# The opening of a two-layer encoder kernel: two more low halves written by DMA, two first scaled tiles on ScalarE, narrow column products among wide ones, and one column sum moved

## What is computed

```python
shift, scale, gate = split(silu(c) @ w_mod[i] + b_mod[i], 3)
h = rmsnorm(x, norm_g[i]) * (1.0 + scale) + shift
# layer 0: z, bg, cg, xh = split(h @ w_in, 4); y = depthwise width-3 conv of cg * xh
#          y = (bg * y * silu(z)) @ w_out
# layer 1: z from h @ w_in, u and v = gelu(rest); v = layernorm(v), mixed over
#          128-position chunks per head; y = (u * sv * silu(z)) @ w_out
x = x + gate * y
```

## Time and profile before

| | |
|---|---|
| median of three runs | 814.75 us |
| profiled execution, its span | 812.9 us |
| TensorE busy | 803.3 us, 99% |
| VectorE busy | 649.2 us, 80% |
| ScalarE busy | 442.6 us, 54% |
| granted TensorE clock | 1.00 until after the last product |
| DMA, first three of 40 slices (61 us) | busy share 0.9 or more |

### The profile page before, as it was taken

One profiled execution on the slowest core, in us unless ns is written; L12 is line 12 of the kernel. 1 busy time (PEld: TensorE's weight loads), 2 busy tenths in 40 slices (PEclk: granted clock), 3 DMA queues, 4 the chain that ended last, 5 costly groups with the idle time before them and its releaser, 6 DMA issues.

```text
span 812.9 us, 15224 instructions
## 1 busy us (share of the span) xinstructions
PE 803.3 (99%) x5614; PEld 752.5 (93%) x5614; DVE 649.2 (80%) x950; ACT 442.6 (54%) x624; POOL 50.9 (6%) x68
## 2 busy tenths in 40 slices
PE   9999999999999999999999999999999999999997
PEld 8779999999999999988889888899999999988896
DVE  5989999999999999898653787567888888897534
ACT  4575656565656666562332844446667677762220
POOL 1010000000000000000000000010000000000000
PEclk9999999999999999999999999999999999999999
DMA  9994566666565656587422162414555445487103
GB/s 350 366 245 131 153 185 179 184 177 190 171 196 166 202 164 198 171 315 288 160 79 79 61 250 98 134 21 143 148 155 148 125 140 148 136 303 265 52 1 104
DMA packets 39566, 137.85 MB, mean 170 GB/s; under 512 B 4336, under 2 KB 6512, under 8 KB 39536
## 3 DMA queue, kind: packets, MB, share of 16 engines
q1 hardware_dynamic: 31616, 110.64, 37.0%
q0 software_dynamic: 6912, 25.17, 16.4%
q10 hardware_dynamic: 1008, 1.66, 0.6%
HBM read 108.09 MB, written 4.19 MB: 138 GB/s over the span
## 4 chain that ended last, share of the span: by engine, by line
PE 94%; DVE 3%; issue 2%; ACT 0%; POOL 0%; POOLq 0%; DVEq 0%; ACTq 0%
PE pp L1190 11%; PE pp L1191 11%; PE pp L1192 11%; PE pp L1046 8%; PE pp L1048 7%; PE pp L1047 7%; PE p_aux L1190 7%; PE p_aux L1192 7%; PE p_aux L1191 7%; PE pp L1328 4%; PE pp L1326 4%; PE pp L1327 4%; PE p_aux L1400 2%; PE pp L1145 1%; PE pp L1062 1%
## 5 line engine op out<-in xcount | busy, mean ns | idle before, releaser
L1190 PE MATMUL pp<-h_hi,wh 128*128 128x256 f32 x280 | 79.3, 283 | 0.0
L1192 PE MATMUL pp<-h_hi,wl 128*128 128x256 f32 x280 | 79.2, 283 | 0.0
L1191 PE MATMUL pp<-h_lo,wh 128*128 128x256 f32 x280 | 79.2, 283 | 0.0
L1701 DVE TENSOR_TENSOR wl<-wt,wh 128x1024 fp32r<-128x1024 f32 x56 | 66.5, 1219 | 0.2 <-ACT wh L698 0.2
L698 ACT ACTIVATE wh<-wt 128x1024 fp32r<-128x1024 f32 x56 | 58.9, 1054 | 13.7 <-DVE wt L1682 7.6
L1190 PE MATMUL pp<-s_hi,wh 128*128 128x256 f32 x224 | 63.4, 283 | 0.0
L1191 PE MATMUL pp<-s_lo,wh 128*128 128x256 f32 x224 | 63.4, 283 | 0.0
L1192 PE MATMUL pp<-s_hi,wl 128*128 128x256 f32 x224 | 63.4, 283 | 0.0
L1192 PE MATMUL p_aux<-s_hi,wl 128*128 128x256 f32 x224 | 63.4, 283 | 0.0
L1191 PE MATMUL p_aux<-s_lo,wh 128*128 128x256 f32 x224 | 63.4, 283 | 0.0
L1190 PE MATMUL p_aux<-s_hi,wh 128*128 128x256 f32 x224 | 63.4, 283 | 0.0
(11 more groups left out here) (237 smaller groups left out, 2598.1 us busy)
## 6 DMA issues: line engine op xcount, KB each, us to landing
raw<-in_stream SPq DMA_DIRECT2D x144, 512.0 KB, 4.0
wl<-raw POOLq DMA_DIRECT2D x28, 512.0 KB, 4.5
raw_l<-in_stream SPq DMA_DIRECT2D x18, 512.0 KB, 4.6
raw_s<-in_stream SPq DMA_DIRECT2D x16, 512.0 KB, 13.6
wl_b<-raw POOLq DMA_DIRECT2D x16, 512.0 KB, 4.5
raw_m<-in_stream SPq DMA_DIRECT2D x14, 512.0 KB, 3.2
x_s<-in_xt SPq DMA_DIRECT2D x4, 512.0 KB, 6.0
w_lo_s<-raw POOLq DMA_DIRECT2D x4, 512.0 KB, 5.4
```

The source lines that it names most:

```text
L1190: pe.matmul(out, hi, hi_of(k), start=fresh and k == 0, stop=False, skip_group_check=not fresh)
L1191: pe.matmul(out, hi, lo_of(k), start=False, stop=False, skip_group_check=not fresh)
L1192: mm = pe.matmul(out, lo, hi_of(k), start=False, stop=k == 3, skip_group_check=not fresh)
L1701: dve.tensor_tensor(wl[par][:, part], wt[par][:, part], f32(wh[par][:, part]), ALU.subtract).then_inc(t_cut, 1)
```

## The change

It makes these edits, all in the opening:

- `BY_DMA` gets tiles 2 and 3: VectorE's two subtractions go, ScalarE makes two more negated copies, GpSimd issues two more DMAs, ahead of the four.
- The first scaled tile of stages 2 and 3 is made by ScalarE (`begin_sum`), and VectorE goes on from the second.
- Stage 1's eight wide direct products (16 passes) go; eight narrow ones (one column each, also 16 passes) stand behind single wide products of stage 0.
- The second sum, `start_columns(1)`, moves into the pair products of stage 0. Of these the ones with tile 2's low part move to stage 1.
- In stage 2 the products with the low part stand last.
- VectorE's order is adapted: the first `h_lo` ahead of the accumulation, `hf` of stage 1 ahead of `start_amp(1)`.

```diff
--- before.py
+++ after.py
@@ -64,8 +64,8 @@
 W_BOUT = W_BUZ
 W_END = W_BOUT + 4 * DPAIRS
 UZ_SLOTS = 4 * PAIRS
-Q_MINUS_W = -4
-BY_DMA = (5, 4, 6, 7)
+Q_MINUS_W = -6
+BY_DMA = (2, 3, 5, 4, 6, 7)
 
 
 
@@ -264,6 +264,7 @@
         sq_ready = sem("sq_ready")
         ms_in, s_used, wide_ready = [sem(f"ms_in{j}") for j in range(S_RING)], sem("s_used"), sem("wide_ready")
         conv_first = sem("conv_first")
+        acc_begun = sem("acc_begun")
         neg_w, w_lo_in = sem("neg_w"), [sem(f"w_lo_in{j}") for j in range(RING)]
         direct_done = sem("direct_done")
         sq_added = sem("sq_added")
@@ -308,7 +309,8 @@
 
             n = CUT_ORDER.index(w)
             earlier = sum(v in BY_DMA for v in CUT_ORDER[n % RING:n:RING])
-            return (w_lo_in[n % RING], 16 * (earlier + 1)) if w in BY_DMA else (consumed, n + 1)
+            by_dve = sum(v not in BY_DMA for v in CUT_ORDER[:n + 1])
+            return (w_lo_in[n % RING], 16 * (earlier + 1)) if w in BY_DMA else (consumed, by_dve)
 
         def s_at(kp, j):
 
@@ -317,12 +319,12 @@
 
         def small(kp):
 
-            if kp < 2:
+            if kp < 1:
                 return [p_small[:, WIDE_AT + WIDE * t:WIDE_AT + WIDE * t + 1] for t in range(4)]
             return [p_small[:, 4 * kp + t:4 * kp + t + 1] for t in range(4)]
 
         def small_pair(kp, first):
-            if kp < 2:
+            if kp < 1:
                 return p_small[:, WIDE_AT:WIDE_AT + 4 * WIDE].rearrange("p (t e) -> p t e", e=WIDE)[:, first:first + 2, 0]
             return p_small[:, 4 * kp + first:4 * kp + first + 2]
 
@@ -642,6 +644,13 @@
             for k in range(KD):
                 act.wait_ge(x_in[k // 2], 16)
                 act.activation(x_squared(k), x_s[:, k, :], ACT.Square).then_inc(sq_ready, 1)
+            def begin_sum(kp):
+                slot, land = s_at(kp, 0)
+                act.wait_ge(ms_in[slot], land)
+                act.wait_ge(acc_used, kp - 1)
+                act.activation(acc_s[:, kp % 2, :], raw_s[:, slot, 0:S], ACT.Copy,
+                               scale=silu_c[:, 0:1]).then_inc(acc_begun, 1)
+
             for kp, before, after in ((0, [0], [2]), (1, [1], []), (2, [3, 5], [4, 6]), (3, [7], [])):
                 if kp == 0:
                     act.wait_ge(consts, 3)
@@ -655,6 +664,8 @@
                 if kp:
                     for w in before:
                         cut_hi_start(w)
+                if kp in (1, 2):
+                    begin_sum(kp + 1)
                 act.wait_ge(amp_ready, kp + 1)
                 h_tiles(0, 0, (2 * kp, 2 * kp + 1), ALL)
                 for w in after:
@@ -1120,6 +1131,12 @@
                                        start=j == 0 and n == 0 and t == 0, stop=False, skip_group_check=True)
                 mm.then_inc(direct_done, 1)
 
+            def narrow_column(n, t):
+
+                slot, land = s_at(1, 0)
+                return pe.matmul(small(1)[t], raw_s[:, slot, S * n + P * t:S * n + P * (t + 1)], silu_c[:, n:n + 1],
+                                 start=n == 0 and t == 0, stop=False, skip_group_check=True)
+
 
             pe.wait_ge(consts, 3)
             keep_clock(WARM[0])
@@ -1134,8 +1151,6 @@
             broadcast(p_rstd[:, :], 2, ALL)
             start_columns(0)
             keep_clock(WARM[2])
-            pe.wait_ge(amp_ready, 1)
-            direct_columns(1, 0)
             for kp in range(4):
                 w = (0, 1, 3, 4)[kp]
                 pe.wait_ge(hi_cut, CUT_ORDER.index(w) + 1)
@@ -1145,34 +1160,63 @@
                     return pe.matmul(pp[2 * b + u][:, :], stationary[:, w % 4, at], moving[:, 2 * kp + n, :],
                                      start=start, stop=stop)
 
-                for n in range(2):
-                    k = 2 * kp + n
-                    pe.wait_ge(h_hi_cut, k + 1)
-                    for s in (w_hi_s, w_lo_s):
-                        if n == 0 and s is w_lo_s:
-                            pe.wait_ge(*low_made(w))
-                        for b in range(2):
-                            for u in range(2):
-                                part(b, u, n, s, h_hi, s is w_hi_s and k == 0, False)
-                    pe.wait_ge(h_cut, k + 1)
+                def high_by_high(n):
+                    pe.wait_ge(h_hi_cut, 2 * kp + n + 1)
                     for b in range(2):
                         for u in range(2):
-                            mm = part(b, u, n, w_hi_s, h_lo, False, k == KD - 1)
-                        if n == 1:
-                            mm.then_inc(blocks, 1)
-                if kp == 0:
-                    start_columns(1)
+                            part(b, u, n, w_hi_s, h_hi, kp == 0 and n == 0, False)
+
+                def low_by_high(n):
+                    pe.wait_ge(*low_made(w))
+                    if kp == 0 and n == 0:
+                        pe.wait_ge(ms_in[s_at(1, 0)[0]], s_at(1, 0)[1])
+                        pe.wait_ge(amp_ready, 1)
+                    for b in range(2):
+                        for u in range(2):
+                            mm = part(b, u, n, w_lo_s, h_hi, False, False)
+                            if kp == 0 and n == 0:
+                                narrow_column(0, 2 * b + u)
+                    return mm
+
+                def high_by_low(n):
+                    pe.wait_ge(h_cut, 2 * kp + n + 1)
+                    for b in range(2):
+                        for u in range(2):
+                            mm = part(b, u, n, w_hi_s, h_lo, False, kp == 3 and n == 1)
+                            if kp == 0 and n == 0:
+                                column = narrow_column(1, 2 * b + u)
+                    if kp == 0 and n == 0:
+                        column.then_inc(direct_done, 1)
+                    return mm
+
+                if kp == 2:
+                    for products in (high_by_high, high_by_low, low_by_high):
+                        for n in range(2):
+                            mm = products(n)
+                else:
+                    for n in range(2):
+                        high_by_high(n)
+                        low_by_high(n)
+                        mm = high_by_low(n)
+                mm.then_inc(blocks, 2)
                 w = (2, 5)[kp // 2]
-                pe.wait_ge(*low_made(w))
+                pe.wait_ge(*((hi_cut, CUT_ORDER.index(w) + 1) if kp == 0 else low_made(w)))
                 for u in range(2):
+                    def bg_part(k, a, h, start=False, stop=False):
+                        at = slice(256 * (k % 4) + P * u, 256 * (k % 4) + P * (u + 1))
+                        return pe.matmul(p_pair[u][:, :], a[:, w % 4, at], h[:, k, :], start=start, stop=stop)
+
                     for n in range(2):
                         k = 2 * kp + n
-                        at = slice(256 * (k % 4) + P * u, 256 * (k % 4) + P * (u + 1))
-                        mm = unit(p_pair[u][:, :], lambda _: (w_hi_s[:, w % 4, at], w_lo_s[:, w % 4, at]),
-                                  rows(h_hi), rows(h_lo), (k,), k == 0, k == KD - 1)
+                        bg_part(k, w_hi_s, h_hi, start=k == 0)
+                        mm = bg_part(k, w_hi_s, h_lo)
+                        if kp:
+                            mm = bg_part(k, w_lo_s, h_hi, stop=k == KD - 1)
+                        if kp == 1:
+                            mm = bg_part(n, w_lo_s, h_hi)
                     if kp % 2:
                         mm.then_inc(blocks, 1)
-                    if u == 0 and kp in (1, 2):
+                    if u == 0 and kp < 3:
                         start_columns(kp + 1)
             pe.wait_ge(xh_used, 2)
             for w in (6, 7):
@@ -1612,35 +1656,36 @@
                 dve.tensor_tensor(amp[:, k:k + 2], amp[:, k:k + 2], cols[:, C_NORM + k:C_NORM + k + 2],
                                   ALU.mult).then_inc(amp_ready, 1)
 
+            def go_on(kp, *kts):
+                start_at[:] = acc_begun, kp - 1
+                start_tiles(kp, *kts)
+
             dve.wait_ge(rstd_bc, 1)
             scale_tile(0, p_rstd[:, :], ALL, 0)
             start_amp(0)
             scale_tile(1, p_rstd[:, :], ALL, 0)
             cut_lo_start(0)
+            cut_h_tile(0, 0, ALL)
             start_tiles(1, 2, 3)
-            cut_h_tile(0, 0, ALL)
-            start_tiles(1, 4)
             cut_h_tile(0, 1, ALL)
-            start_tiles(1, 5, 6, 7)
-            cut_lo_start(2)
-
+            start_tiles(1, 4, 5, 6, 7)
+
+            scale_pair(1, p_rstd[:, :], ALL, 0)
             start_amp(1)
-            scale_pair(1, p_rstd[:, :], ALL, 0)
             cut_lo_start(1)
+            go_on(2, 1)
             cut_h_tile(0, 2, ALL)
-            start_tiles(2, 0)
+            start_tiles(2, 2)
             cut_h_tile(0, 3, ALL)
-            start_tiles(2, 1, 2, 3, 4, 5, 6, 7)
+            start_tiles(2, 3, 4, 5, 6, 7)
             scale_pair(2, p_rstd[:, :], ALL, 0)
 
             start_amp(2)
-            cut_lo_start(3)
-            start_tiles(3, 0)
```

(6 more changed lines are left out.)

## The result

The changed kernel takes 817.38 us, the median of 7 runs (816.93 to 817.80), and the kernel before 814.98 beside it: 1.003 times as long, interval 1.002 to 1.004, or 2.40 us slower. That is 0.3% and above the 816.4 from which the prediction speaks of slower. The forecast was 817.0. The profiled execution took 817.02 us with a span of 814.7, 1.8 more than before.

The account below looks back on a forecast made before the run. TensorE, busy 99% of the span, bounds the kernel, so the shift of stage four's start from 50.08 counts. Part 4 decides it: median 814.75 + 2.3 = 817.0 us, range 815.9 to 818.6, chance 0.50.

Parts of the forecast that it names:

- Parts 1 to 3: Opening before stage four: narrow passes, second sum among pair products, VectorE relieved; stage four could start at 49.6, -0.5 us.
- part 1: Stage one: starts at 19.56 (-0.87 us), eight narrow products cost +1.88, so it ends +1.01 us.
- Part 4: Two more low halves by DMA: tile 6 lands about 47.1, stage four starts at 52.1 to 52.6, +2.3 us.
- not later than this: Tile 4's DMA, landing near 51 and wanted at 53, was to add nothing to stage four's +2.3 us.
- part 3: Stages two and three: VectorE relieved, waits of 0.83 and 0.50 us go, stage four could start at 49.6, -0.5 us.
- A: Rival, opening: the DMA engines absorb the new DMAs and part 3 stands: -0.5 us, 814.2 us; chance 0.28.
- B: Rival, stage one: narrow passes hide under wide products, -2.4 us, 812.4 us, if the DMAs are absorbed too; chance 0.07.
- C: Rival: the wait before stage four grows and TensorE's clock falls, +4.3 us or so, 819.2 us; chance 0.15.

Follow-up runs that it names:

- the copies behind: The changed kernel with ScalarE's copies of tiles 6 and 7 placed behind the tiles of stage four, not ahead: 817.36 us, 1.0027 to the kernel before.

## Why the prediction was right

**Parts 1 to 3 held, to 0.13 us or less.** Forecast and measured: stage one 19.56 and 19.56, narrow product 0.235 (0.24 by its rows) and 0.23 us, second sum 27.93 and 27.84, stage two 30.38 and 30.25, third sum 37.6 and 37.58, stage three 40.4 and 40.33. The run with the narrow products alone took 0.93 us more, against part 1's +1.01.

**Part 4 had the right mechanism.** ScalarE waits for `raw`, tile 6 lands at 47.2 (forecast 47.1), the last copy ends at 51.0 (51.1), tile 5 makes TensorE wait 0.58 (0 to 1.1). Stage four came at 51.94, at the edge of the forecast's bounds (51.9 to 53.3), so +1.86 against +2.3; the step to the end was +1.87 with nothing given back. With the DMAs away and the narrow products kept, stage four is at 50.23; the reverse, it is at 51.82. So the DMAs set it.

**What was off inside it.** An idle time of 2 us or more was to stand ahead of tile 6's copies. It stood ahead of tile 4's (2.66 us), and only 0.57 ahead of tile 6's: the forecast had tile 4 negated at about 45 and asked nothing of its transfer, which came at 44.6. It changes nothing at the end, as tile 4's copies are over at 46.6 and tile 6 lands behind that. Tile 2's low half was to be there by 32, with the stream slipping behind it. It landed at 34.26, and the stream went first: tile 3 was on ScalarE at 32.13, forecast 33.7. The order was wrong, and so was the reason: SP's queue holds tiles 4 and 6 back until that landing, which the prediction doesn't mention. The engines' total work was nearly right, and tile 6 hangs on the total: their share is 1.0 or more in every microsecond from 20 to 46. An adding DMA took 2.6 us of them (67.4% of 2 us for 0.27 MB, 97.3% for 0.39), not 2.8. Tile 3's low half came at 43.3, forecast 41.5 to 42.7, with 44.16 wanted. The Trainium skill, DMA: Bandwidth & Descriptors, section Anatomy of one DMA — SWDGE (gpsimd) path, gives a constant and a rate from which 3.2 us follow for each, an estimate; the six of the opening took 5.7 to 8.9, median 8.4, and the measurement decides. The same page, section Queues, rings and completion order, says that an engine takes turns between the queues it has work for, packet by packet. About equal bytes from 31 to 33 agree. That the new queue got none until 29.5, though its issue was over at 26.6, doesn't follow from it, nor do 0.39 against 0.07 MB from 43 to 45 with tile 6 in flight; why, no run shows.

**What I had wrong.** The sentence that tile 4's DMA is "not later than this". In the changed kernel it lands at 52.7 and is wanted at 52.95, so it is hidden by 0.2 us only; with the copies behind, it is the next wait, 1.29 us. Whoever had repaired only the order of ScalarE's copies would have won nothing. And the -0.5 us for part 3 without part 4 wasn't reached by any run with VectorE's subtractions back (50.23 and 50.20 instead of 49.6); in those runs VectorE has the work again, so the -0.5 itself wasn't tried. It is likely too much by 0.2, as stage three took 5.65 us in its new order and not the 5.44 of the sum.

**Rivals.** A stood for one DMA and fell for two. B fell with the 0.23 us of a narrow product. C did not happen where I put it: the clock stayed at 1.00 at stage four.

**Where luck came in.** The median rose by 2.40 us and stage four by 1.86 only, so that 817.38 lies so near 817.0 is in part luck: the mechanism was over-priced by 0.4, and 0.5 us came from elsewhere. Some 0.2 of them lie outside the span. The prediction added a constant 1.85 for it; time less span is 2.23 to 2.32 us in the seven executions of the changed kernel and 1.86 to 2.20, median 2.1, in the 87 of the kernel before that ran beside the experiments. All kernels with new DMAs have medians near 2.3, those without at most 2.2; the cause is open. The rest lies in the span, whose median rose by 2.2 (815.1 against 812.9) and not 1.86. One execution, that of the kernel with the copies behind, shows what can lengthen it. Last broadcast of the program, changed kernel:

```profile
808.54 0.71 PE L1113 MATMUL p_aux<-work,ones 128*128 128x128 f32 x4
```

and the kernel with the copies behind, with its window:

```profile
808.63 1.11 PE L1113 MATMUL p_aux<-work,ones 128*128 128x128 f32 x4
```

```profile
809.00:810.00 1.00, 0.73 (x4) 0.44 (x3) 0.23 (x1) 0.00 (x0) 0.00 (x0) 0.50 0.00 0
```

At 0.50 (1.2 GHz) the same four products take 0.4 us longer, and VectorE starts behind them at 809.77 instead of 809.29. Spans of the changed kernel's other executions reach 815.5, that one at the lowest mean clock (0.996). That their longer spans are this tail is an inference: they have no trace.

## What to carry to other kernels

Handing an engine's work to the DMA engines is free only as long as they have holes before the next thing that is waited for; count the engines' total time (here, worked out from rows, 2.6 to 2.8 us for an adding 512 KB, 1.28 for a plain one) against the hole, since the first was absorbed and the second cost 2.1 us. When a wait goes, look for the second consumer of the same late stream before promising its length. And split a bundle: the one cheap edit in it, 0.7 us moved to an idle engine, was worth -0.88 us alone.

## What the runs showed of the hardware

Two adding DMAs that were issued while the stream filled the engines (25.56 and 34.43) moved nothing for 3.9 and some 3.6 us. Then the first shared by bytes (0.27 and 0.28 MB in 2 us) while taking 67% of the engines against 37%; from 43 to 45 the adding DMAs got 0.39 MB against 0.07. From issue to landing the first three took 8.3 to 8.9 us. A float32 product of one column between wide ones costs 0.23 us, in both places where these kernels have it. And the clock at the last broadcast differs between executions of like kernels, 0.71 or 1.11 us for the same four products.
